# First attention laid between the groups of the latent product, a cheaper inverse, other squares, another load order

## The reference

```
h = rms_norm(x); z = h @ w_in -> q_a, k_a, v_a, c_q, c_kv, k_rope
q_a, k_a: rms_norm per head (8 and 2 heads of 64)
o_a = softmax(q_a k_a^T / 8 + bias[t5_bucket(rel)] | window 128 | sink) v_a     # first attention
q  = rms_norm(c_q) @ w_qb    -> 8 heads of 64 + 32, norm per head, rope on 32
kv = rms_norm(c_kv) @ w_kvb  -> 8 heads of 64 + 64, norm per head on k
o_b = softmax((q_nope k_nope^T + q_rot k_rot^T) / sqrt(96)) v                   # latent attention
x = x + [rms_norm(o_a), rms_norm(o_b)] @ w_o
x = x + expert_choice_ffn(rms_norm(x))     # 16 experts, 3 matrices of 1024x1024 each
```

## Time and profile before

| | us |
|---|---|
| median of the runs | 1501.07 |
| the profiled execution's own time | 1504.31 |
| its span | 1502.3 |
| TensorE busy | 1261.3 (84%) |
| VectorE busy | 695.3 (46%) |
| ScalarE busy | 461.9 (31%) |
| DMA: 369.61 MB, mean | 246 GB/s |
| mean granted clock of TensorE (share of full speed) | 0.875 |

### The profile page before, as it was taken

One profiled execution on the slowest core, in us unless ns is written; L12 is line 12 of the kernel. 1 busy time (PEld: TensorE's weight loads), 2 busy tenths in 40 slices (PEclk: granted clock), 3 DMA queues, 4 the chain that ended last, 5 costly groups with the idle time before them and its releaser, 6 DMA issues.

```text
span 1502.3 us, 21971 instructions
## 1 busy us (share of the span) xinstructions
PE 1261.3 (84%) x8802; PEld 897.6 (60%) x8802; DVE 695.3 (46%) x1149; ACT 461.9 (31%) x665; POOL 271.3 (18%) x290
## 2 busy tenths in 40 slices
PE   7957897888868887886976768999969978899997
PEld 4535654343324333333844757999959756799996
DVE  2666445221212121123355646766763265477676
ACT  4333322111111011012423315434343332444342
POOL 0000045732032130331314410000016420000000
PEclk9986687787988788888898988999989967899998
DMA  6761187999999999999485123545344300354451
GB/s 255 285 280 56 50 343 329 430 427 430 428 427 429 428 430 428 428 429 403 179 332 219 57 84 113 210 172 200 144 168 168 128 13 15 126 196 181 184 193 42
DMA packets 36000, 369.61 MB, mean 246 GB/s; under 512 B 4070, under 2 KB 5615, under 8 KB 12271
## 3 DMA queue, kind: packets, MB, share of 16 engines
q1 hardware_dynamic: 33552, 364.66, 59.8%
q10 hardware_dynamic: 2398, 4.27, 0.8%
HBM read 367.84 MB, written 1.06 MB: 246 GB/s over the span
## 4 chain that ended last, share of the span: by engine, by line
PE 56%; DMA 26%; DVE 9%; POOL 3%; issue 3%; ACT 3%; DVEq 0%; SPq 0%; ACTq 0%; POOLq 0%
PE ps L642 54%; DMA ring<-in_w_up 23%; DVE W L2088 2%; DMA ring<-in_ada_w 2%; PE ps L657 1%; ACT ring_parts L487 1%; DVE XH L2047 1%; DMA ring<-in_w_in 1%; DVE W L2361 1%; PE ps L887 1%; DMA ring<-in_s_out 1%; DMA ring<-in_fox_in 1%; DVE ring_parts L2119 0%; POOL ring_parts L495 0%; DVE ss L1861 0%
## 5 line engine op out<-in xcount | busy, mean ns | idle before, releaser
L642 PE MATMUL ps<-W_parts 128*128 128x256 f32 (+1 forms) x2672 | 391.0, 309 | 8.0 <-issue 4.3
L642 PEld LDWEIGHTS ps<-W_parts 128*128 128x128 f32 x2672 | 363.3, 194 | 34.6 <-issue 10.2
L642 PE MATMUL ps<-ring,W 128*32 128x512 f32 x1536 | 225.9, 737 | 74.4 <-DMA ring<-in_w_up 44.0
L642 PE MATMUL ps<-W 128*32 128x64 f32 (+6 forms) x1696 | 159.4, 325 | 37.2 <-DVE W L2369 24.5
L642 PEld LDWEIGHTS ps<-ring,W 128*32 128x32 f32 x1536 | 52.4, 128 | 226.5 <-issue 156.1
L495 POOL TENSOR_TENSOR ring_parts<-ring,ring_parts 128x2048 fp32r<-128x2048 f32 x18 | 98.7, 5497 | 362.9 <-ACT ring_parts L487 327.0
L642 PEld LDWEIGHTS ps<-W 128*32 128x32 f32 (+4 forms) x1696 | 103.1, 173 | 95.8 <-issue 83.5
L2395 DVE TENSOR_TENSOR W_parts<-ring,W_parts 128x2048 fp32r<-128x2048 f32 x44 | 100.9, 2293 | 29.8 <-ACT W_parts L1591 29.8
L642 PE MATMUL ps<-XH_parts,ring_parts 128*128 128x256 f32 x512 | 94.3, 287 | 8.5 <-issue 5.0
L2276 DVE COPY W<-ps 128x1024 f32<-128x1024 f32 x16 | 19.6, 1225 | 171.1 <-PE ps L642 171.1
L642 PE MATMUL ps<-ring_parts,W_parts 128*128 128x512 f32 (+1 forms) x288 | 87.2, 411 | 10.5 <-DVE W_parts L2384 10.5
(11 more groups left out here) (363 smaller groups left out, 1447.1 us busy)
## 6 DMA issues: line engine op xcount, KB each, us to landing
ring<-in_w_gate SPq DMA_DIRECT2D x32, 2048.0 KB, 21.8
ring<-in_w_up SPq DMA_DIRECT2D x32, 2048.0 KB, 26.5
ring<-in_w_down SPq DMA_DIRECT2D x32, 2048.0 KB, 23.0
ring<-in_ada_w SPq DMA_DIRECT2D x24, 2048.0 KB, 11.2
ring<-in_up SPq DMA_DIRECT2D x44, 1024.0 KB, 5.6
ring<-in_dn SPq DMA_DIRECT2D x44, 512.0 KB, 3.5
ring<-in_fox_in SPq DMA_DIRECT2D x6, 2048.0 KB, 7.7
ring<-in_w_in SPq DMA_DIRECT2D x2, 2048.0 KB, 13.6
```

The source lines that it names most:

```text
L642: return pe.matmul(o, l, r, start=a, stop=z_, skip_group_check=True, **kw)
```

## The change

1. The first attention moves ahead of and between the groups of the latent product. TensorE: `scores(0)`, then the transposes of c_q and c_kv, `ada_product(1)`, group 0 of the latent product, and in each step s = 0 to 3 also groups 2s+1 and 2s+2. Both only have two banks each now (`score_a`: banks 0 and 1, the groups: banks 2 and 3), so that the scores of step s+1 wait for the maxima of s, and group g for the copy of g-2. After step 3 come the transposes of the heads (two banks, each waits for the copy two before it), with `ada_product(2)` and `(3)` between; then steps 4 to 7 with `ada_product(4)`, `(5)` and `ada_turn(0)` between.
2. `inverse`: a RECIPROCAL of 4 columns and a copy that spreads them over 256.
3. ScalarE squares q and k while it copies the groups out of PSUM (a second ACTIVATE for each), and scales q_a by a prepared column `aqs`; k_a's copy moves to ScalarE as well. The table of Exp is loaded ahead of the first step, and again after each Sqrt between.
4. The squares of the outputs are added over 4 chunks by VectorE (`squares_summed`), so that 4 products with the ones remain.
5. `wo_high` and `wo_low` now stand in steps 4 to 6 and behind, in halves of both loads; `wo_rows` waits for each half by itself. `ada_copy(0)` and `ada_keep(0)` stand behind `spread_copied(7)`.
6. `xgl` moves from GpSimd to VectorE, ahead of the wait for the transposed routing weights.
7. The load of `ada` 4 (slot 3) is issued ahead of `w_o` 0.

```
-    load("w_o", 1, apart=True, to=4)
-    load("ada", 1, to=3)
+    load("ada", 1, to=3)
+    load("w_o", 1, apart=True, to=4)
...
+            pe.wait_ge(S("qa_copied"), 2)
+            pe.wait_ge(S("ka_copied"), 1)
+            pe.wait_ge(S("line_spread"), 16)
+            scores(0)
+            c_turn()
+            ada_product(1)
+            latent_product(0)
+            for s in range(4):
+                turn_probs(2 * s)
+                turn_probs(2 * s + 1)
+                spread(s)
+                if s < 3:
+                    scores(s + 1)
+                latent_product(2 * s + 1)
+                pe.wait_ge(S("r_copied"), s + 1)
+                outputs(2 * s)
+                outputs(2 * s + 1)
+                if s < 3:
+                    latent_product(2 * s + 2)
+            for g in range(4):
+                heads_turn(g)
+            ada_product(2)
+            ada_product(3)
+            for g in range(4, 8):
+                heads_turn(g)
...
+            exponentials(0)
+            latent_copied(0)
+            for s in range(4):
+                spread_copied(s)
+                if s == 2:
+                    act.wait_ge(S("qkv_var"), 1)
+                    act.activation(rs24[:, :, 0:16], ss24[:, :, 0:16], ACT.Sqrt).then_inc(S("qkv_std"), 1)
+                latent_copied(2 * s + 1)
+                if s < 3:
+                    exponentials(s + 1)
+                    latent_copied(2 * s + 2)
...
+                own(v.reciprocal(den[:, u, a], den[:, u, a]))
                 if s >= 2:
                     v.wait_ge(S("r_turned"), s - 1)
-                v.reciprocal(rin[:, s % 2, :].rearrange("p (h d) -> p h d", h=4), bcast(den[:, u, a], [P, 4, 64])
-                             ).then_inc(S("rin_ready"), 1)
+                v.tensor_copy(rin[:, s % 2, :].rearrange("p (h d) -> p h d", h=4), bcast(den[:, u, a], [P, 4, 64])
+                              ).then_inc(S("rin_ready"), 1)
...
+            maxima(0)
+            k_rotated(0)
+            k_rotated(1)
+            for s in range(4):
+                inverse(s)
+                probs_copied(2 * s)
+                probs_copied(2 * s + 1)
+                if s < 3:
+                    maxima(s + 1)
+                if s < 2:
+                    q_sums(s)
...
+                if s >= 2:
...
+                    q_normed(s - 2)
+                normalized(s)
...
             def low_between(s):
-                if s < 4:
-                    wo_low(s // 2, s % 2)
-                if s == 5:
+                if s < 7:
+                    wo_low(*((0, 0), (1, 0), (0, 1))[s - 4])
+                if s == 6:
                     o_low(0)
+                if s == 7:
+                    squares_summed(0)
...
+            v.wait_ge(S("rows_high"), 1)
+            tt(xgl, XNf, xgh.bitcast(F32), ALU.subtract).then_inc(S("rows_low"), 1)
             v.wait_ge(S("route_mm"), 2)
```

More of the change, by code:

```diff
@@ L807, in _, with c_turn @@
[L807 to L812 removed]
+            def c_turn():
+                pe.wait_ge(S("latent_normed"), 2)
+                for j in range(5):
+                    for t in range(NT):
+                        o = (j % 2) * T + t * P
+                        last = pe.transpose(ps[:, (5, 2, 3)[j // 2], o:o + P],
+                                            z[:, t, Z_CQ + j * P:Z_CQ + j * P + P], ident)
+                    if j in (1, 3, 4):
+                        last.then_inc(S("c_turned"), 1)
@@ L815, in _ @@
                                   wq[:, c, 384 * n:384 * n + 384], c == 0, c == 2)
[L816 to L823, removed]
+                else:
+                    wk = filled("qkvb", 1)[:, 0:2 * 1024].rearrange("p (c n) -> p c n", c=2)
@@ L824, in _ @@
                     for c in range(2):
-                        last = mm(ps[:, (4, 5, 6, 0)[2 * t + n], :], cT[:, 3 + c, t * P:t * P + P],
+                        last = mm(ps[:, 2 + g % 2, :], cT[:, 3 + c, t * P:t * P + P],
                                   wk[:, c, BANK * n:BANK * n + BANK], c == 0, c == 1)
[L827 to L832, removed]
+                last.then_inc(S("qkv_mm"), 1)
@@ L910, in outputs, with attention @@
                 last.then_inc(S("pv_mm"), 1)
-            def attention(first, between):
+            def attention(first, last_, between):
                 scores(first)
                 scores(first + 1)
-                for s in range(first, first + 8):
+                for s in range(first, last_):
                     turn_probs(2 * s)
@@ L919, in attention @@
                     spread(s)
-                    if s < first + 6:
+                    if s + 2 < last_:
                         scores(s + 2)
@@ L1403, in _, with qa_copied, latent_copied @@
                           ).then_inc(S("line_spread"), 16)
-            act.wait_ge(S("z_var"), 2)
-            act.activation(rs13[:, :, 10:13], ss13[:, :, 10:13], ACT.Sqrt).then_inc(S("z_std"), 1)
-            for t in range(NT):
+            def qa_copied(t):
                 act.wait_ge(S("qa_turned"), t + 1)
                 act.activation(qTa[:, :, t * P:t * P + P], ps[:, t, :].rearrange("p (i t) -> p i t", i=4), ACT.Copy,
[L1409 to L1417, removed]
+                               scale=aqs[:, 0:1]).then_inc(S("qa_copied"), 1)
+            def latent_copied(g):
                 act.wait_ge(S("qkv_mm"), g + 1)
@@ new lines, in _ @@
+            act.wait_ge(S("aqs_ready"), 1)
+            qa_copied(0)
+            act.wait_ge(S("z_var"), 2)
+            act.activation(rs13[:, :, 10:13], ss13[:, :, 10:13], ACT.Sqrt).then_inc(S("z_std"), 1)
+            qa_copied(1)
+            act.wait_ge(S("ka_turned"), 1)
+            act.activation(kTa[:, :], ps[:, 4, 0:T], ACT.Copy, scale=C("ak")).then_inc(S("ka_copied"), 1)
+            own(act.activation(warm[:, :], ident[:, 0:1], ACT.Exp))
+            for j in range(5):
+                act.wait_ge(S("c_turned"), j // 2 + 1)
+                act.activation(cT[:, j, :], ps[:, (5, 2, 3)[j // 2], (j % 2) * T:(j % 2) * T + T], ACT.Copy,
+                               scale=C("cq", j) if j < 3 else C("ckv", j - 3)).then_inc(S("c_copied"), 1)
@@ L1979, in rotate @@
                 return tt(o2, r[:, 2], r[:, 3], ALU.add)
[L1981 to L1996, removed]
@@ L2046, in maxima @@
                             bias = nf[:, 8 * half + h, 0:T] if t else nf[:, 8 * half + h, T:T + P]
-                        last = v.tensor_tensor_reduce(Pex[:, h, 0:n], score(h, n), bias, 1.0, -3e38, ALU.add, ALU.max,
+                        last = v.tensor_tensor_reduce(Pex[:, h, 0:n], score_a(h) if u < 2 else score(h, n), bias,
+                                                      1.0, -3e38, ALU.add, ALU.max,
                                                       mx[:, u, h:h + 1])
@@ new lines, in _ @@
+            k_sums(0)
+            k_sums(1)
+            ts(ss24[:, :, 16:24], ss24[:, :, 16:24], 1.0 / NOPE, EPS, ALU.mult, ALU.add
+               ).then_inc(S("qkv_var"), 1)
+            v.wait_ge(S("qkv_std"), 2)
+            own(v.reciprocal(ss24[:, :, 16:24], rs24[:, :, 16:24]))
+            for t in range(NT):
+                kh = kv[:, t, :].rearrange("p (h d) -> p h d", h=BH)[:, :, 0:NOPE]
+                tt(kB[:, t, :, 0:NOPE], kh, bcast(ss24[:, t, 16:24], [P, BH, NOPE]), ALU.mult)
+                last = v.tensor_copy(kB[:, t, :, NOPE:BQ], krot[:, t, :].unsqueeze(1).to_broadcast([P, BH, ROPE]))
@@ L2114, in wo_low @@
+            last.then_inc(S("latent_normed"), 1)
+            for g in range(4):
+                v.wait_ge(S("qkb_turned"), 4 + g + 1)
+                t, h = g // 2, 4 * (g % 2)
+                ts(kTb[0:BQ, h:h + 4, t * P:t * P + P],
+                   ps[0:BQ, 2 + g % 2, :].rearrange("p (h t) -> p h t", h=4), C("kbg")[0:BQ], None, ALU.mult
+                   ).then_inc(S("kb_copied"), 1)
             def wo_low(i, half):
```

184 lines of the change are left out of this document (98 added, 86 removed).

## The result

The changed kernel takes 1463.98 us (median of four runs, 1462.86 to 1468.09) against 1502.66 for the kernel before in the same comparison: ratio 0.9738, 95% interval 0.9698 to 0.9778, 38.7 us faster. The forecast was 24.6 us faster, with a range down to 1464; the time fell just out of it on the fast side. The profiled execution of after (1468.09) is the slowest of its four; its span is 1466.3, 36.0 less than before, and I account for those 36.0.

What follows compares the result with a forecast made beforehand. The attention was taken as a chain between engines whose holes could hold the latent product. Gains 14.5 (attention) + 2.8 (squares) - 0.7 (xgl) + 8.0 (fox) = 24.6 off 1501.1 gave 1476.5 us, range 1464 to 1492.

Steps and rivals of the forecast that it cites:

- The new wait: Start of the first attention: scores(0) waits for the bias line's read, landing at 67.8; TensorE stands about 11 us.
- From there to step 4: First attention, steps 0 to 3 and heads: step 4's transposes start at 121.5 against 140.3 before, 18.8 us earlier.
- TensorE sets the pace: Steps 0 to 3 of the first attention: TensorE's 6.6 us per step exceeds ScalarE's 4.5 and VectorE's about 5.3.
- Steps 4 to 7: First attention's second half: 36.0 us against 31.7, added products and w_o splits outweighing 5.1 saved by the inverse.
- Fox: Fox's attention: each of eight waits for the inverse shrinks by 1.28 us or by itself; 8 us gained.
- behind the attention: After the first attention: fewer products with the ones gain 2.8 us; xgl on VectorE loses 0.7.
- xgl: Routing: xgl's subtraction on VectorE, ahead of the top-k, loses 0.7 us, at worst 2.3.
- Squares: Behind the attention: products with the ones fall from 32 instructions to 8, 3.73 us to 0.9; 2.8 gained.
- Table loads: First attention: added ScalarE table switches cost the load alone, 1.28 us each; the skill's extra drain given one in ten.
- all at full clock: Rival, chance 0.15: interleaved work keeps TensorE's clock up, attention over at 142.3, 39.8 us gained in all, 1461.

Runs made afterwards that it cites:

- a_order_only: The changed kernel with the old inverse, xgl back on GpSimd and the 16 products with the ones back: 1497.61 us, ratio 0.9966.
- The filler: The kernel before, old inverse kept, with three unread products ahead of TensorE's wait for the inverse in each step of fox's attention: 1498.06 us, ratio 0.997.
- b_inverse: The kernel before with only the new inverse (RECIPROCAL of 4 columns, then a spreading copy), in both attentions: 1475.15 us, ratio 0.9817.

## Why the prediction was right and wrong

- *The new wait.* Right: 67.8 forecast, 69.5 measured in a run whose issue was 1.2 us later. The stand itself was 15.4 us and not 11: I let it begin behind the transposes of c, but those now come behind the scores that wait. It was priced as a fact of the new order and not asked for its remedy.
- *From there to step 4.* Right in size: 121.5 forecast, 121.1 measured, and the pace of 6.6 us of TensorE work was 7.2 to 7.4. But the reason "TensorE sets the pace" only holds with the short inverse; `a_order_only` shows 8.7 to 9.9 without it.
- *Steps 4 to 7.* 36.0 forecast, 33.9 measured at a clock of 0.75, against 0.61. The late w_o load, counted as nothing with "0 to 4" if late, cost ScalarE 1.13 us; it waited 1.0 to 1.15 us in the other five kernels of the new order too.
- *Fox.* This step failed, in size: "each of the eight waits shrinks by 1.28 or by itself" gave 8.0, measured 14.2. I took the wait off and left the clock at its old value, although I had read that low clock as a sign of a chain full of holes. The waits for the inverse in fact shrank by less, 5.8 us (to 4.8, where I had said some 2), and the clock, which I had put at nothing, made the same 209 instructions 8.7 us shorter in all. The filler shows that the clock saves time by itself, 4.4 us. The same is missing from "behind the attention": the w_o products gained 3.5 us in `b_inverse` with no edit of theirs.
- *xgl.* This step failed, in sign: 0.7 lost forecast, 4.6 gained measured. I bounded the cost of the added VectorE instruction from 0.7 to 2.3 and never asked what the removed GpSimd instruction was holding up. The added one is about what I said: in after the top-k begins 14.6 us behind the w_o products, 14.0 before. The scan is 4.3 us shorter. Rows of before had it side by side: a subtraction of 4.50 us and a scan of 4.94 started 0.1 us apart.
- *Squares.* 2.8 forecast, 3.3 measured with the wide interval above; in the traces the products themselves give 2.7.
- *Table loads.* The drain of 1.38 us that the Trainium skill (ScalarE: Activation LUTs, "What ACT_TABLE_LOAD costs") gives was not seen: 0.02 us again.
- *The parts.* By themselves: inverse 27.4, order 4.9, xgl 4.6, and squares 3.3 when taken out of the changed kernel, sum 40.2, against 38.7 together. My split was 13.1 for the inverse and 9.4 for the order in the front. In the front alone the inverse gave 15.5 us in the old order, where I had 5.1, and the new order 7.3 with the old inverse, where I had 9.4. Together they gave 17.0, so they overlap, and that my 14.5 came near it is in part luck. By the table the miss is 6.2 in fox, 4.1 in the routing, 2.5 in the front and 1.9 in the w_o products, less 3.7 in the experts and the state space stage, which I can put down to no part of the change. That is 11.5 for the profiled executions with 0.5 in the rest; the medians, which lie 14.1 from the forecast's gain, add 2.6.
- The rival *all at full clock* gave 1461, near the time, by luck and for a partly right reason. The interleaved part did run at 0.96, with either inverse. But the attention ended at 155.0 and not at its 142.3, and what made up for most of that is fox and the routing, for which it had no more than my own numbers.

## What to carry to other kernels

A wait that comes once per step in a chain between engines costs its length and, when it lets TensorE's clock fall, a share of all TensorE work around and behind it; price both, by the stretch's granted clock. When work moves off GpSimd or VectorE, look first at what ran beside it with two operands in SBUF. When a step moves ahead, list what it needs that used to be there long before, and move that too: here a read of 18 us ate 13 us of the new order.

## What the runs showed of the hardware that I had not expected

- A RECIPROCAL of 128x256 takes 1.74 us and a copy of the same shape 0.29; of 128x4 it takes 0.18. Inverting before spreading is 3.7 times as fast.
- Useless products made a stage faster: 24 of them in fox's attention, clock 0.66 to 0.92, 46.3 to 41.9 us.
- VectorE instructions of 0.68, 0.41 or (two together) 1.29 us took 4.94, 4.54 or 5.20 beside one GpSimd subtraction of 4.5 us, and whether the first or the second was held up hung on 0.1 us.
- The read of 1.5 MB took 15.7, 18.4 or 22.6 us. In the last, one more 2 MB load was issued beside it than in the second; in the first, two of the four went out only in its last microsecond.
